# Expert weights in runs of 16 KB, token rows gathered in quarters and turned by VectorE

## What is computed

```
def moe_ffn(h, w_rg, b_rg, w_re, b_re, w_g, w_u, w_d):
    ...
    xb = h_pad[slot_tok].reshape(n_blk, EXPERT_BLOCK, D)
    def run(args):
        xe, e = args
        return (jax.nn.silu(xe @ w_g[e]) * (xe @ w_u[e])) @ w_d[e]
    ...
    y_assign = yb[dest].astype(jnp.float32) * flat_w[order][:, None]
    return jax.ops.segment_sum(y_assign, tok_sorted, num_segments=N).astype(h.dtype)
```

## Time and profile before

| | before |
|---|---|
| median of 3 runs | 950.09 us (949.8 to 951.06) |
| profiled execution, first to last instruction | 949.8 us |
| mean granted TensorE clock | 1.000 |
| busy: PE / PEld / DVE / ACT / POOL | 928.6 / 469.4 / 547.0 / 195.0 / 61.6 us |
| DMA in the whole span | 260.57 MB, mean 274 GB/s |
| DMA from 640 to 700 us | 25.18 MB, mean 420 GB/s |
| expert part (first `gate_up` to last weights) | 412.8 to about 871 us |

### The profile page before, as it was taken

The page is one execution under the profiler, slowest core; times in us unless marked ns, Lnnn a source line. Parts: engine busy times, 40 slices in busy tenths (PEclk is TensorE's granted clock), DMA queues, the critical chain, the costliest instruction groups (busy, mean ns, idle before and its releaser), DMA issues.

```text
span 949.8 us, 11382 instructions
## 1 busy us (share of the span) xinstructions
PE 928.6 (98%) x4433; PEld 469.4 (49%) x4433; DVE 547.0 (58%) x1126; ACT 195.0 (21%) x428; POOL 61.6 (6%) x70
## 2 busy tenths in 40 slices
PE   9999999999999999999999999999999999999997
PEld 5565778876554445634343434334334333334443
DVE  3106442547877311664787787787777575768434
ACT  3111211004746202311111111111111111111401
...
DMA  9690354140004792779999999999999999999211
GB/s 309 203 310 0 102 176 150 53 147 1 1 1 116 234 371 105 294 270 405 419 419 418 419 419 421 419 418 419 420 420 419 419 419 420 419 422 402 99 44 50
DMA packets 74874, 260.57 MB, mean 274 GB/s; under 512 B 12554, under 2 KB 36502, under 8 KB 49956
## 3 DMA queue, kind: packets, MB, share of 16 engines
...
...
## 4 chain that ended last, share of the span: by engine, by line
PE 80%; SPq 12%; DMA 4%; DVE 2%; POOL 1%; issue 1%; ACT 0%; DVEq 0%
PE ps L1127 72%; SPq L378 12%; DMA w<-in_w_exp_down 3%; PE ps L1508 2%; PE ps L1778 1%; PE ps L1151 1%; DMA h<-in_x_prompt 1%; DMA mixT<-in_state_conv 1%; PE ps L1813 1%; PE ps L1511 0%; PE ps L1317 0%; PE ps L1248 0%; DVE probs L2344 0%; PE ps L1333 0%; POOL gk L718 0%
## 5 line engine op out<-in xcount | busy, mean ns | idle before, releaser
L1127 PE MATMUL ps<-w,xe 128*64 128x512 f32 x1024 | 229.0, 596 | 9.4 <-DMA w<-in_w_exp_up 8.2
L2718 DVE TENSOR_TENSOR h<-h,ps 128x1024 f32<-128x1024 f32 x120 | 143.2, 1215 | 109.4 <-PE ps L1127 109.3
L1127 PEld LDWEIGHTS ps<-w,xe 128*64 128x64 f32 x1024 | 69.8, 137 | 149.6 <-issue 131.8
L1127 PE MATMUL ps<-w,hT 128*64 128x512 f32 x504 | 115.4, 599 | 0.6 <-DMA w<-in_w_exp_down 0.6
L1127 PE MATMUL ps<-yk,ST 128*128 128x512 f32 (+1 forms) x320 | 105.3, 431 | 0.7 <-DVE yk L2708 0.5
L1127 PE MATMUL ps<-xT,wring 128*128 128x272 f32 x384 | 100.4, 401 | 0.0
L1127 PEld LDWEIGHTS ps<-xT,wring 128*128 128x128 f32 x384 | 68.6, 190 | 24.9 <-issue 12.2
L1127 PE MATMUL ps<-wring,xT 128*32 128x128 f32 (+2 forms) x368 | 77.9, 404 | 0.6 <-DVE xT L2013 0.4
L1127 PEld LDWEIGHTS ps<-yk,ST 128*128 128x128 f32 (+1 forms) x320 | 48.6, 174 | 56.9 <-issue 26.7
L1075 ACT ACTIVATE sg<-ps 64x256 f32<-64x256 f32 x64 | 24.1, 377 | 253.6 <-PE ps L1127 243.0
L758 POOL DMA_INDIRECT xg<-hn_rows,sidx x32 | 32.0, 998 | 645.6 <-PE ps L1778 369.7
...
## 6 DMA issues: line engine op xcount, KB each, us to landing
...
```

The lines of the kernel that those rows point to most:

```text
L1127: return nc.tensor.matmul(out, l, r, start=start, stop=stop, skip_group_check=skip)
L2718: TTn(h[0:r, t, :], h[0:r, t, :], both(b, r), ALU.add).then_inc(S["hadd"], 1)
```

## The change

Four things are changed together.

1. The rows of an expert's matrices are dealt to partitions in another order, "(p k c)" in place of "(k p c)", so that the two halves of a partition lie side by side in HBM: 16 KB in one run. For experts 0 to 7 the six pieces of 1 MB remain (8 KB runs, which now lie 16 KB apart). From expert 8 on there are three DMAs of 2 MB with runs of 16 KB, gate and up after all of `gate_up(J-3)`, and `gate_up(J)` waits at part 0 for all of gate and up.
2. A gather fetches quarters of rows, 1 KB each, with two indirect DMAs for each expert in place of one (slots 0 to 31 and 32 to 63); `sidx` has two columns for each expert, and eight small instructions write it in place of two.
3. VectorE turns the gathered quarters in blocks of 32x32 (`V.transpose`) from `xg` to `xe`, waits for that, and multiplies by the gain in place (`gmix`; `gex` and its DMA are gone). `rows_T` with its four TensorE transposes is gone, and bank 3 serves `hidden_T` alone. GpSimd's wait on `x_tr` is now for VectorE.
4. In VectorE's round, `x_columns(J+1)` comes behind `add(J-2, 1)` and `add(J-2, 2)`, and `spots(J-1)` behind `low_rows(J-1)`. Silu and the product with up read their PSUM columns in another order.

```diff
-        xe = at("xe", [P, 2, 4, P], 72 * K)
+        xe = at("xe", [P, 2, DC, SLOTS], 72 * K)
...
-        gex = small("gex", [P, 2, 4])
...
-        sidx = small("sidx", [P, JOBS], I32)
-        icur = small("icur", [P, 1], I32)
+        sidx = small("sidx", [P, JOBS, 2], I32)
+        icur = small("icur", [P, 2], I32)
...
-        WGU = [a[f"w_exp_{x}"].rearrange("e (k p c) n -> e p k (c n)", k=2, c=4) for x in ("gate", "up")]
-        WD = a["w_exp_down"].rearrange("e (k p c) n -> e p k (c n)", k=2, c=2)
+        WGU = [a[f"w_exp_{x}"].rearrange("e (p k c) n -> e p k (c n)", k=2, c=4) for x in ("gate", "up")]
+        WD = a["w_exp_down"].rearrange("e (p k c) n -> e p k (c n)", k=2, c=2)
         G0, G1, D0, D1, U0, U1 = range(6)
         SOURCE = [(WGU[0], 0), (WGU[0], 1), (WD, 0), (WD, 1), (WGU[1], 0), (WGU[1], 1)]
-        PLACE = [(0, 1, 2, 3, 4, 5), (2, 4, 0, 1, 3, 5), (0, 2, 4, 5, 1, 3)]
+        PLACE = [(0, 1, 2, 3, 4, 5), (2, 3, 0, 1, 4, 5), (0, 1, 4, 5, 2, 3)]
...
+        FULL = 8
+        WHOLE = [x.rearrange("e p k n -> e p (k n)") for x in (WGU[0], WD, WGU[1])]
+        def load_whole(sp, k, e):
+            slot, at_ = e % 3, PLACE[e % 3][2 * k]
+            sp.dma_start(W[slot][:, at_:at_ + 2, :].rearrange("p k n -> p (k n)"), WHOLE[k][e]).then_inc(S[f"wl{slot}{'ada'[k]}"], 16)
+        def whole(J):
+            return isinstance(J, int) and J >= FULL
+        def of_half(r0, k):
+            return ps[r0:r0 + SLOTS, 0, :].rearrange("s (p k c) -> s k p c", k=2, c=2)[:, k]
         def slot_of(J):
             return J % 3 if isinstance(J, int) else OVSLOT
-        def landings(J):
-            return 32 * (J // 3 + 1) if isinstance(J, int) else J * 32 + 32 * (NOV0 + 1 - NE)
+        def landings(J, kind):
+            if kind == "a":
+                return 32 * (J // 3 + 1) if isinstance(J, int) else J * 32 + 32 * (NOV0 + 1 - NE)
+            held = 16 if kind == "d" and slot_of(J) == 2 else 0
+            if not isinstance(J, int):
+                regular_ = sum((0 if kind == "b" else 16) if whole(i) else 32 for i in range(OVSLOT, NE, 3))
+                return J * 32 + regular_ + 32 - 32 * NE
+            return sum((0 if kind == "b" else 16) if whole(i) else 32 for i in range(J % 3, J + 1, 3)) - held
...
-            return 16 * (J // 2 + 1) if isinstance(J, int) else J * 16 + 16 * (NE // 2 + 1 - NE)
+            return 32 * (J // 2 + 1) if isinstance(J, int) else J * 32 + 32 * (NE // 2 + 1 - NE)
...
+                if whole(J):
+                    sp.wait_ge(S["gu_done"], 2 * (J - 3) + 2)
+                    load_whole(sp, 0, J)
+                    load_whole(sp, 2, J)
+                    return
...
                 sp.wait_ge(S["d_done"], J - 2)
+                if whole(J):
+                    load_whole(sp, 1, J)
+                    return
...
-                pool.indirect_dma_start(out=xg[:, two(J), :], out_offset=None, in_=hn_d.rearrange("n (k d) -> (n k) d", k=2),
-                                        in_offset=bass.IndirectOffsetOnAxis(ap=at, axis=0), bounds_check=2 * N - 1,
-                                        oob_is_err=False).then_inc(S[f"gath{two(J)}"], 16)
+                for k in range(2):
+                    pool.indirect_dma_start(out=xg[:, two(J), 256 * k:256 * k + 256], out_offset=None,
+                                            in_=hn_d.rearrange("n (q d) -> (n q) d", q=4),
+                                            in_offset=bass.IndirectOffsetOnAxis(ap=at[:, k:k + 1], axis=0), bounds_check=4 * N - 1,
+                                            oob_is_err=False).then_inc(S[f"gath{two(J)}"], 16)
             for J in range(NE):
                 if J >= 2:
                     pool.wait_ge(S["x_tr"], J - 1)
-                gather(J, sidx[:, J:J + 1])
+                gather(J, sidx[:, J, :])
             nov = overflow_jobs(pool)
             def gather_job(J):
                 pool.wait_ge(S["hadd"], J * NU)
-                nc.gpsimd.tensor_copy(icur[:], sidx[:, bass.ds(J, 1)]).then_inc(S["ic_ok"], 1)
+                nc.gpsimd.tensor_copy(icur[:].unsqueeze(1), sidx[:, bass.ds(J, 1), :]).then_inc(S["ic_ok"], 1)
                 nc.gpsimd.tensor_copy(jcur[:, 0:1], cst[:, bass.ds(J + C_SL, 1)]).then_inc(S["ic_ok"], 1)
                 nc.gpsimd.tensor_copy(jcur[:, 1:2], wsl[:, bass.ds(J, 1)]).then_inc(S["ic_ok"], 1)
                 pool.wait_ge(S["ic_ok"], J * 3 - 3 * (NE - 1))
                 pool.sem_inc(S["passed"], 1)
-                gather(J, icur[:, 0:1])
+                gather(J, icur[:, :])
...
             def gated(J):
...
-                    last = A(sg[k * SLOTS:(k + 1) * SLOTS, b, :], ps[0:SLOTS, 0, k * 256:(k + 1) * 256], ACT.Silu)
+                    last = A(sg[k * SLOTS:(k + 1) * SLOTS, b, :].rearrange("s (p c) -> s p c", c=2), of_half(0, k), ACT.Silu)
...
-            def rows_T(J):
-                pe.wait_ge(S[f"gath{two(J)}"], gathered(J))
-                if not isinstance(J, int):
-                    pe.wait_ge(S["hT_ok"], J)
-                    pe.sem_inc(S["passed"], 1)
-                elif J >= 2:
-                    pe.wait_ge(S["hT_ok"], J - 1)
-                elif J:
-                    pe.wait_ge(S["xT_done"], J)
-                else:
-                    pe.wait_ge(S["f_pl"], 6)
-                v = xg[:, two(J), :].rearrange("r (p c) -> r p c", c=4)
-                for c in range(4):
-                    last = T(ps[:, 3, c * P:(c + 1) * P], v[:, :, c], eye(P))
-                last.then_inc(S["x_tr"], 1)
...
                         pe.wait_ge(S["hm_ok"], J)
-                if part % 2 == 0:
-                    pe.wait_ge(S[f"wl{slot}{'ab'[half]}"], landings(J))
+                if part == 0:
+                    pe.wait_ge(S[f"wl{slot}a"], landings(J, "a"))
+                elif part == 2 and not whole(J):
+                    pe.wait_ge(S[f"wl{slot}b"], landings(J, "b"))
                 for c in range(2 * part, 2 * part + 2):
                     j = c % 4
                     for k, i in enumerate(((G0, U0), (G1, U1))[half]):
-                        last = mm(ps[k * SLOTS:(k + 1) * SLOTS, 0, :], xe[:, b, j, half * SLOTS:(half + 1) * SLOTS],
+                        last = mm(ps[k * SLOTS:(k + 1) * SLOTS, 0, :], xe[:, b, c, :],
                                   W[slot][:, PLACE[slot][i], j * 512:(j + 1) * 512], c == 0, c == DC - 1, True)
                 if part % 2:
                     last.then_inc(S["gu_done"], 1)
             def hidden_T(J):
                 pe.wait_ge(S["hm_ok"], J + 1)
-                if not isinstance(J, int):
-                    pe.wait_ge(S["xT_done"], J + 1)
-                elif J + 1 < NE:
-                    pe.wait_ge(S["xT_done"], J + 2)
+                if isinstance(J, int):
+                    if J:
+                        pe.wait_ge(S["hT_ok"], J)
+                    else:
+                        pe.wait_ge(S["f_pl"], 6)
                 else:
                     pe.wait_ge(S["hT_ok"], J)
-                if not isinstance(J, int):
...
-                if J + 1 < NE:
-                    rows_T(J + 1)
...
                 dve.wait_ge(S["sl_ps"], k + 1)
-                TS(sidx[0:SLOTS, j0:j0 + n], ps[0:SLOTS, bank, 0:n], 2.0, 2.0 * NOROW, ALU.mult, ALU.add)
-                TS(sidx[SLOTS:P, j0:j0 + n], ps[0:SLOTS, bank, 0:n], 2.0, 2.0 * NOROW + 1.0, ALU.mult, ALU.add).then_inc(S["ix_ok"], 1)
+                for q in range(4):
+                    for k in range(2):
+                        last = TS(sidx[32 * q:32 * q + 32, j0:j0 + n, k], ps[32 * k:32 * k + 32, bank, 0:n], 4.0, 4.0 * NOROW + q, ALU.mult, ALU.add)
+                last.then_inc(S["ix_ok"], 1)
...
+                dve.wait_ge(S["f_ple"], 6)
...
                 b = two(J)
-                dve.wait_ge(S["x_tr"], J + 1)
+                dve.wait_ge(S[f"gath{b}"], gathered(J))
                 if not isinstance(J, int):
                     dve.wait_ge(S["gu_done"], J * 2)
                 elif J >= 2:
                     dve.wait_ge(S["gu_done"], J * 2 - 2)
-                TTn(xe[:, b, :, :].rearrange("p c (k s) -> p c k s", k=2), ps[:, 3, :].rearrange("p (c k s) -> p c k s", k=2, s=SLOTS),
-                    gex[:].rearrange("p k c -> p c k").unsqueeze(3).broadcast_to([P, 4, 2, SLOTS]), ALU.mult).then_inc(S["xT_done"], 1)
+                V.transpose(xe[:, b, :, :].rearrange("p c (k s) -> p c k s", k=2),
+                            xg[:, b, :].rearrange("p (k s c) -> p c k s", k=2, c=DC)).then_inc(S["x_tr"], 1)
+                dve.wait_ge(S["x_tr"], J + 1)
+                TTn(xe[:, b, :, :], xe[:, b, :, :], gmix[:].unsqueeze(2).broadcast_to([P, DC, SLOTS]), ALU.mult)\
+                    .then_inc(S["xT_done"], 1)
...
             def times_up(J):
...
-                    x = sg[k * SLOTS:(k + 1) * SLOTS, b, :]
-                    last = STT(x, x, w[k * SLOTS:(k + 1) * SLOTS, :], ps[SLOTS:2 * SLOTS, 0, k * 256:(k + 1) * 256], ALU.mult, ALU.mult)
```

(11 more changed lines are left out.)

9 lines of the change are left out of this document (3 added, 6 removed).

## The result

| | before | changed |
|---|---|---|
| median, measured side by side | 951.06 us (5 runs) | 955.59 us (5 runs, 953.61 to 956.03) |
| ratio | | 1.0047 (1.0036 to 1.0058) |
| profiled execution | 949.8 us | 953.7 us |
| gate_up(31) starts | 856.62 | 860.69 |

The changed kernel is slower by 0.47%. The range held the time. The likeliest case (950.8 for the profiled execution) missed it by 2.9 us, on the slower side.

What follows compares the result with a forecast made beforehand. The DMA stream of weights was taken as the bound: +2.0 + 0.5 - 5.2 + 4.28 - 0.58 = +1.0 us, so span 950.8 and median 951.1 us. Range 945.0 to 956.5; the forecast's own 948.2 to 952.0.

Steps and rivals of the forecast that it cites:

- list, second gather, turning: Ahead of gate_up(0): six more list instructions +1.1, second indirect DMA +1.33, VectorE's turning 0.45 less; +2.0 us.
- runs of 16 KB and quarters in the stream: Weight stream: fewer packets save 0.22 us a round, -5.2 us; extra gather packets in experts 0 to 7, +0.5.
- coarser landings: At gate_up(31): waiting for all of gate and up, landing at 860.90 against a start at 856.62, costs +4.28 us.
- gate_up(31) to the end: Behind gate_up(31): the wait for D(30) goes, -0.58 us.
- The bound: Expert part's end: start of the DMA stream, plus its bytes at its rate, plus TensorE's work behind the last weights.
- TensorE's saving: Dropping rows_T saves 0.39 us a round, but from about expert 15 this becomes waiting for weights: worth 0.
- From landing to gate_up(0): First gather's landing to gate_up(0): VectorE's transpose and multiplication take 1.5 us, 0.45 less than TensorE and VectorE now.
- The step on VectorE: VectorE's round: xe just met at 6.6 us, spots ends near 12.0 before combine(J-1, 0) wants it at 13.6; cost 0.
- rival 1: Stream: 16 KB runs bring little, 0 to 0.17 us a round; 952.3 to 956.3 us; chance 0.30.
- Rival 2: Stream: 16 KB runs bring more, 0.35 to 0.64 us a round; 941 to 948 us; chance 0.20.
- Rival 3: VectorE becomes the bound if V.transpose takes over 1.6 us; at 2.2 us the end is 967 us; chance 0.05.
- Rival 4: Start hardly later, list or second gather hidden: -1 us, 950; chance 0.43 together with the forecast.

Runs made afterwards that it cites:

- e2: Kernel before, with only gate_up from expert 8 on waiting at part 0 for all of gate and up, runs still 8 KB: ratio 1.0021.
- e1: Kernel before plus only the 16 KB runs and their coarse wait; gathered rows keep their old order, so products are mismatched: ratio 0.9981.
- e3: Kernel before, with only the first load of expert 3 waiting for all of gate_up(0) instead of half: ratio 1.0030.
- e11: Changed kernel with VectorE's round in the whole order of before (x_columns right behind times_up, spots ahead of add 3): ratio 1.0050.
- e10: Changed kernel with matmuls on constants (16 instructions of 0.43 us) filling TensorE's idle time ahead of gate_up(0): ratio 1.0059.
- e7: Changed kernel with only VectorE's spots back in its old place ahead of add 3: ratio 1.0041.

## Why the prediction was right, and where it was wrong

The terms of the sum, for the profiled executions:

| term | predicted | measured | from |
|---|---|---|---|
| front of the kernel, untouched | 0 | +0.77 | 409.77 - 409.00 |
| list, second gather, turning | +2.0 | +1.96 | gate_up(0) |
| first issue behind gate_up(0) | 0 | +1.43 | 5.12 - 3.69 |
| runs of 16 KB and quarters in the stream | -5.2 + 0.5 = -4.7 | -4.03 | changed - e2 |
| coarser landings | +4.28 | +3.94 | e2 - before |
| gate_up(31) to the end | -0.58 | -0.17 | 93.01 - 93.18 |
| sum | +1.0 | +3.90 | 953.7 - 949.8 |

Runs and quarters stand in one row because the prediction's 0.22 us a round has the packets of the second gather in it. Measured apart, the runs are -5.41 (e1 - e2) and the quarters +1.38 (changed - e1).

**What held.** The bound: a stream of weights that starts late and then decides. e3 and e11 show it from both sides. TensorE's saving was worth nothing, and the waits went to the first matmul. The coarse landing was within 0.34 us. The start was within 0.04, although two of its parts were off: V.transpose is 0.45 us longer than the nearest row, and the gather landed 0.46 us sooner behind its last issue. That these two nearly cancelled is luck. The cost of a packet came out at 8.7 ns where the two stretches of the old trace had given 10.5: right in kind, a fifth too high.

**What failed.** The largest miss is a term that the sum put at nothing. The step "From landing to gate_up(0)" counted the transposes that went as time saved. They were also TensorE's only work between the projections and gate_up(0). Without them it stood idle for 3.90 us, gate_up(0) ran in part at half clock, and the first issue behind it moved by 1.43 us. Scatter of the front gave another 0.77.

In the stream 0.67 us of the forecast gain are missing. The cost of a packet is one part of it. The count of packets was off too: the prediction had a gather in quarters bring five packets and a completion more on each engine, and the queue of the gathers has 4592 packets instead of 4080 in the whole run, which is one more for each of 32 gathers on each of 16 engines. So the packets of the quarters cost next to nothing, and yet the quarters' stream is 1.38 us longer than that of e1 (0.80 in e10, whose first issue stands as close behind gate_up(0) as in e1). Most of it is in the pace of the late rounds. It is not the late landing at expert 23, since halves have such a landing as well. What it is stays open.

Behind gate_up(31) the coarse wait gave back 1.02 us (e2), more than the 0.58 forecast, and VectorE took some 0.85 of it back: combine(29, 0) waits 0.80 us for VectorE's last work of the round. The step on VectorE checked combine(J-1, 0) in an ordinary round, and not in the last one, where it stands right behind half a gate_up. Putting spots back (e7) does not help, because `low_rows` then ends last.

**Rivals.** The time lies in the interval of rival 1 (952.3 to 956.3), and its condition is nearly met: what the changed kernel gained in the stream is 4.03 us over 23 rounds, 0.175 us a round, on the border of 0.18 that the prediction drew. But this explains only 0.67 us of the 2.9 by which the time was missed; most of it is the clock and the front, which no rival had named. A time alone would have "confirmed" rival 1. Rival 2 is false (0.235 us at most, not 0.35). Rival 3 did not happen at 1.15 us for V.transpose; e11 shows that in the old order of VectorE the rounds grow to 14.3 us and even that doesn't move the end. Rival 4 is false in both halves: the start was not hidden, and the packets were cut as the change says. The range had held 945.0 to 956.5, and the measured 955.59 is 0.9 from its edge. "Same" had the largest chance (0.43); what came is "slower" by the prediction's own 0.2%, with 0.37.

**Open.** Why the stream with quarters runs 0.09 us a round slower in the late rounds. What makes one landing 1 to 2 us late once in each of these streams; the packet of the queue "instruction" is a candidate. How much of the lost clock could be bought back by filling of the right length. And the 0.4 us between medians and spans.
